# Half of an output projection moved into the delta rule's prologue, with partial sums kept in DRAM

## The chip, the core and the metric

The kernel runs on one core of a Trainium2 chip. The metric is the device time of one execution in microseconds (us). Engines: PE is TensorE (PEld its weight loads), DVE VectorE, ACT ScalarE, POOL GpSimd, and SP SyncE, which here only issues transfers; each of them takes its instructions in the order in which the program has them.

## What is computed

Block one mixes a sequence of 512 latent positions (and 256 context positions) with a state space part (SSD) and a gated delta rule (GDN), and ends with an output projection, a norm and a gated residual. Block two starts from that. Cut to what matters here:

```
def merge(ssd_y, gdn_o, z, dtype):
    y = jnp.concatenate([ssd_out_norm(ssd_y, z[..., :SSD_WIDTH], ssd_norm_w),
                         gdn_out_norm(gdn_o, z[..., SSD_WIDTH:], gdn_norm_w)], axis=-1)
    return rms_norm(y.astype(dtype) @ w_out, post_w)
h_lat = h_lat + gate_l[:, None] * merge(ssd_l, gdn_l, z_l, h_lat.dtype)
...
hn = rmsnorm(h, e_norm[j])
u = hn @ e_w_in[j]
```

D is 2048. The first 1024 rows of `w_out` meet the SSD half of y, the last 1024 rows the GDN half. SSD is finished before GDN begins.

## The kernel before

**Stages.** The program is a row of stages with a barrier of all engines between them: `ssd_stage`, then `gdn_stage` (from 1076.7 us of the span), then `even_stage` (from 1459.2 us), whose first part is block one's output projection. Tiles are [128 partitions, ...]; y lies in DRAM as 16 blocks of 128 channels x 512 positions, 256 KB each (`y1[0:8]` from SSD, `y1[8:16]` from GDN).

**The projection.** `Projection` computes jobs: a job is 128 output columns, a sum over KD = 16 steps of 128 rows. Operands are split into a high and a low part, so that a step is three matmuls of 128x512: hi*hi, hi*lo, lo*hi. Weights come in chunks of four steps (128x512, 256 KB), through a ring of buffers: SP loads chunk m into `w`, ACT writes the high part `w_hi` (`split_high`, which waits for the load and for PE to be done with the chunk one ring before), DVE subtracts to get `w_lo` (`split_low`), PE multiplies and counts `chunk_done`. Two PSUM accumulators alternate, so job n can start only when job n-2 was evacuated.

**even_stage** has 16 such jobs called "mix" (`MixedInput` holds what surrounds them), with a ring of 8. SP's order is in `MixedInput.load`: chunks and the 16 y blocks, alternating, through a ring of four y buffers, then `h` (4 MB), two tables, then the further chunks. ACT and DVE split each y block (`x_hi`, `x_lo`), and PE waits for block k in job 0. For each job ACT first runs `split_high` 8 chunks ahead of the job's last chunk, then squares the accumulator and copies it times a gain into `mixed[n]`; DVE sums the squares in `total`. A matmul with ones turns it into the norm (`pe_mixed`), and then DVE goes over the 16 blocks: mixed*inv, h+mixed, and the low part of u, block by block, with block two's first three jobs behind it on PE.

**gdn_stage** handles eight heads in four pairs. Its prologue prepares the first two heads (`norms`, `turn_v`, `turn_k`, `products` on PE, `squares`, `norms`, `decay`, `copy`, `queries` on ACT, `norms`, `decayed` on DVE), squares and norms of heads 2 and 3, and a triangular inverse of 96 blocks of 32x32: SP gathers them through DRAM (`gather`, `blocks_load`), DVE runs 31 dependent steps (`triangle`), ACT transposes (`turn_tri`), SP writes them out and spreads them (`scatter`, 4 and 16 transfers). PE's first matmul of the main loop (`level5_t`, L361) waits for the spread. From there the four pairs run; they are not touched by the change.

How far the three engines run ahead of PE is in `sp_upto`, `act_upto` and `dve_upto`: at step s SP loads chunks up to s's chunk + 2*ring and stores every job that is done, ACT splits up to s's chunk + ring and then evacuates the jobs that are done, DVE subtracts up to s's chunk + ring. Since a split of chunk m waits for PE to be done with chunk m-ring, an engine that is asked for `chunk(s) + ring` stands still until PE has come to step s.

## Time and profile before

| | us |
|---|---|
| runs (3) | 4012.24, 4014.65, 4020.4; median 4014.65 |
| profiled execution, span from first to last instruction | 4017.9 |
| PE busy in it | 3635.5 (90%) |
| DVE busy | 1998.8 (50%) |
| ACT busy | 1513.7 (38%) |
| prologue of gdn_stage, first instruction to first L361 | 1076.7 to 1163.6 |
| mix part of even_stage, first matmul to last | 1464.2 to 1658.3 |

The profiled execution is listed with its span only; a time of its own beside it is not given, and the span lies within the three runs. Busy PE means that some matmul is in the array or its end is modelled there; what a matmul costs in a dense row is read from their count over a stretch, not from the duration of one. Times on the trace are from the start of the span.

### The profile page before, as it was taken

How to read it: one execution, taken by the hardware profiler on the slowest of the kernel's cores; microseconds unless marked ns; L12 is line 12 of the kernel's file. 1: busy time of each engine (PE TensorE's matmuls, PEld its weight loads, DVE VectorE, ACT ScalarE, POOL GpSimd, SP SyncE). 2: the span in 40 equal slices, each digit the busy share in tenths (PEclk: the TensorE clock that was granted, in tenths of full speed). 3: DMA queues.
4: the chain of work that ended last, by engine and by line, in shares of the span. 5: the costliest groups of instructions: out<-in, count | busy, mean ns of one | idle time of the engine just before them, and what ended most of it. 6: DMA issues, size and time to landing. Idle time of an engine off the chain costs nothing. (4 is left out here: it accounts for less than half of the span.)

```text
span 4017.9 us, 50439 instructions
## 1 busy us (share of the span) xinstructions
PE 3635.5 (90%) x20182; PEld 2995.2 (75%) x20182; DVE 1998.8 (50%) x3101; ACT 1513.7 (38%) x2512; POOL 430.6 (11%) x334
## 2 busy tenths in 40 slices
PE   6699999899647679999999879999999899989998
PEld 2288888787546558778888768787899788867786
DVE  6554555464567533555555553445533344444454
ACT  1322222244545343455655642323222344432332
POOL 1000000042221000011101140020000000013011
PEclk8899999899878889999999989999999999999999
DMA  9344343223232253233322253335755667633332
GB/s 353 123 159 130 103 134 108 87 54 104 97 100 83 64 160 102 89 111 90 94 84 82 61 160 97 92 97 90 121 118 116 103 107 105 108 87 115 92 91 88
DMA packets 585417, 437.91 MB, mean 109 GB/s; under 512 B 63734, under 2 KB 519874, under 8 KB 583904
## 3 DMA queue, kind: packets, MB, share of 16 engines
q1 hardware_dynamic: 578272, 414.88, 39.4%
q10 hardware_dynamic: 6048, 19.14, 1.2%
q8 instruction: 159, 2.61, 0.3%
q0 software_dynamic: 864, 0.67, 0.1%
q14 instruction: 74, 0.61, 0.0%
HBM read 381.31 MB, written 53.26 MB: 108 GB/s over the span
## 5 line engine op out<-in xcount | busy, mean ns | idle before, releaser
L1913 DVE TENSOR_TENSOR w_lo<-w,w_hi 128x512 fp32r<-128x512 f32 x446 | 303.7, 697 | 598.3 <-ACT w_hi L1906 598.3
L1906 ACT ACTIVATE w_hi<-w 128x512 fp32r<-128x512 f32 x446 | 272.8, 626 | 586.0 <-PE od_acc L1892 177.5
L3670 PE MATMUL ta_acc<-ta_x_hi,w_hi 128*128 128x512 f32 x1024 | 404.5, 395 | 13.6 <-DVE ta_x_lo L3810 8.2
L3780 DVE TENSOR_TENSOR w_lo<-w,w_hi 128x512 fp32r<-128x512 f32 x260 | 207.4, 800 | 407.2 <-ACT w_hi L3698 405.5
L3671 PE MATMUL ta_acc<-ta_x_lo,w_hi 128*128 128x512 f32 x1024 | 401.8, 392 | 0.0
L3672 PE MATMUL ta_acc<-ta_x_hi,w_lo 128*128 128x512 f32 x1024 | 401.4, 392 | 0.0
L3698 ACT ACTIVATE w_hi<-w 128x512 fp32r<-128x512 f32 x260 | 164.1, 631 | 507.0 <-PE ta_acc L3672 474.9
L1890 PE MATMUL od_acc<-od_u_hi,w_hi 128*128 128x512 f32 x768 | 306.1, 399 | 11.3 <-DVE w_lo L1913 10.5
L1890 PE MATMUL ev_acc<-ev_u_hi,w_hi 128*128 128x512 f32 x680 | 282.6, 416 | 31.2 <-DVE ev_u_lo L2637 19.7
L1892 PE MATMUL od_acc<-od_u_hi,w_lo 128*128 128x512 f32 x768 | 300.4, 391 | 0.0
L1891 PE MATMUL od_acc<-od_u_lo,w_hi 128*128 128x512 f32 x768 | 300.3, 391 | 0.0
L1891 PE MATMUL ev_acc<-ev_u_lo,w_hi 128*128 128x512 f32 x680 | 269.6, 396 | 0.0
L1892 PE MATMUL ev_acc<-ev_u_hi,w_lo 128*128 128x512 f32 x680 | 268.9, 396 | 0.0
L3670 PEld LDWEIGHTS ta_acc<-ta_x_hi,w_hi 128*128 128x128 f32 x1024 | 194.2, 190 | 55.5 <-issue 12.0
L1377 PE MATMUL p_acc<-u_hi,p_w_hi 128*128 128x512 f32 x576 | 228.4, 396 | 7.5 <-DVE p_w_lo L1489 7.5
L1384 PE MATMUL p_acc<-u_hi,p_w_lo 128*128 128x512 f32 x576 | 228.6, 397 | 0.0
L1378 PE MATMUL p_acc<-u_lo,p_w_hi 128*128 128x512 f32 x576 | 225.0, 391 | 0.0
L3672 PEld LDWEIGHTS ta_acc<-ta_x_hi,w_lo 128*128 128x128 f32 x1024 | 194.3, 190 | 41.1
L3671 PEld LDWEIGHTS ta_acc<-ta_x_lo,w_hi 128*128 128x128 f32 x1024 | 194.3, 190 | 40.5 <-issue 0.5
L1534 DVE TENSOR_TENSOR p_w_lo<-p_w,p_w_hi 128x1024 fp32r<-128x1024 f32 x68 | 83.0, 1223 | 242.6 <-ACT p_w_hi L1432 242.6
L1890 PEld LDWEIGHTS ev_acc<-ev_u_hi,w_hi 128*128 128x128 f32 x680 | 130.3, 192 | 72.5 <-DVE w_lo L1913 14.6
L1890 PEld LDWEIGHTS od_acc<-od_u_hi,w_hi 128*128 128x128 f32 x768 | 145.2, 189 | 44.5 <-DVE w_lo L1913 11.3
(640 smaller groups left out, 8081.8 us busy)
## 6 DMA issues: line engine op xcount, KB each, us to landing
w<-in_o_w_in_dram SPq DMA_DIRECT2D x260, 256.0 KB, 8.1
p_w<-in_w_in_dram SPq DMA_DIRECT2D x72, 512.0 KB, 4.9
w<-in_e_w_in_dram SPq DMA_DIRECT2D x144, 256.0 KB, 2.9
mod_w<-in_w_ada_dram SPq DMA_DIRECT2D x8, 4096.0 KB, 23.9
w<-in_ple_gate_w_dram SPq DMA_DIRECT2D x128, 256.0 KB, 2.8
gate_w<-in_w_ada_dram SPq DMA_DIRECT2D x16, 1024.0 KB, 6.0
z_w<-in_w_in_dram SPq DMA_DIRECT2D x64, 256.0 KB, 2.9
w<-in_e_w_out_dram SPq DMA_DIRECT2D x64, 256.0 KB, 2.8
```

What stands on the lines that cost most here:

```text
L1377: pe.matmul(lat, wh, x_hi[:, k, :], start=first, stop=False)
L1378: pe.matmul(lat, wh, x_lo[:, k, :], start=False, stop=False)
L1384: last = pe.matmul(lat, wl, x_hi[:, k, :], start=False, stop=end)
L1890: pe.matmul(out, hi, self.x_hi[:, k, :], start=first, stop=False)
L1891: pe.matmul(out, hi, self.x_lo[:, k, :], start=False, stop=False)
L1892: last = pe.matmul(out, lo, self.x_hi[:, k, :], start=False, stop=end)
L1906: act.activation(self.w_hi[m % self.ring][:], self.w[m % self.ring][:], ACT.Copy).then_inc(self.hi_set, 1)
L1913: eng.tensor_tensor(self.w_lo[m % self.ring][:], self.w[m % self.ring][:], self.w_hi[m % self.ring][:].bitcast(F32), ALU.subtract).then_in ...
L3670: pe.matmul(bank, hi, hi_x[:, k, :], start=(k == 0), stop=False)
L3671: pe.matmul(bank, hi, lo_x[:, k, :], start=False, stop=False)
L3672: last = pe.matmul(bank, lo, hi_x[:, k, :], start=False, stop=(k == job.kd - 1))
L3780: dve.tensor_tensor(w_lo[m % RING][:], w[m % RING][:], w_hi[m % RING][:].bitcast(F32), ALU.subtract).then_inc(lo_set, 1)
```

## The change

Eight of the 16 steps of every mix job, those for the SSD half of y, leave even_stage and go into gdn_stage's prologue, as 16 jobs of 8 steps called `mix` (a second `Projection`, with a ring of 4 and the banks 0 and 1). PE does them in portions between the prologue's parts (`MIX_AT` gives the step up to which it goes at each place). ACT evacuates each of these jobs into `mx_out`, SP stores it to a DRAM tensor `mix_part` (16 x 256 KB). In even_stage the 16 blocks of `mix_part` are loaded into `mixed[n]`, DVE adds the accumulator of the other 8 steps to them, ACT squares the sum, and the gain moves into the later multiplication on DVE. The y tiles, weight buffers and outputs of the new jobs lie where `y_m1`, `qdec2`, `qdec3`, `z_in` and others lie later, so these loads and a memset now stand behind the last store. The prologue's operations themselves are the same.

```diff
+MIX = KD // 2
+MIX_AT = (8, 16, 24, 32, 40, 48, 56, 72, MIX * KD)
...
+        with ExitStack() as early:
+            def split(part):
+                return early.enter_context(nc.sbuf_tensor(f"mx_y_{part}", [P, MIX, LAT], F32R))
+
+            y_hi, y_lo = split("hi"), split("lo")
+            y_in = [early.enter_context(nc.sbuf_tensor(f"mx_y_in{i}", [P, LAT], F32)) for i in range(2)]
+            mix = Projection(nc, early, "mx", (y_hi, y_lo),
+                             [Job("plain", w_mix, P * n, mix_part[n], stores=True, kd=MIX) for n in range(KD)],
+                             4, None, acc=[[bank[0]], [bank[1]]], ahead=4)
+            mix.buffers(nc, early, "mx")
...
+        def by_job(upto, eng, step):
+
+            while eng_at[upto.__name__] < step:
+                eng_at[upto.__name__] = min(step, (eng_at[upto.__name__] // MIX + 1) * MIX)
+                upto(eng, eng_at[upto.__name__])
+
+        eng_at = {"sp_upto": 0, "act_upto": 0}
+        mix_at = dict(zip(("norms", "v0", "k0", "kq0", "v1", "k1", "kq1", "sums", "rest"), MIX_AT))
...
+            def load_y(k):
+                if k >= 2:
+                    sp.wait_ge(mix.x_set, k - 1)
+                sp.dma_start(y_in[k % 2][:], y_ready[k]).then_inc(y_loaded[k % 2], 16)
+
             for hd in range(2):
                 load_kq(hd)
+            mix.load_weights(sp, 1)
...
+            for k in range(2):
+                load_y(k)
+            mix.load_weights(sp, 4)
             for hd in range(2):
                 load_qdec(hd)
             for hd in range(2, 4):
...
-            load_z(0)
+            for k in range(2, MIX):
+                load_y(k)
+            by_job(mix.sp_upto, sp, mix_at["kq0"])
             gather(0)
             load_kq(2)
             load_v(2)
+            by_job(mix.sp_upto, sp, mix_at["kq1"])
             gather(1)
             blocks_load(0)
             load_kq(3)
             load_v(3)
+            by_job(mix.sp_upto, sp, mix_at["rest"])
+            mix.wait_stored(sp)
+            load_z(0)
             for hd in range(2, 4):
                 load_qdec(hd)
...
             norms(0)
+            mix.pe_upto(pe, mix_at["norms"])
             for hd in range(2):
                 turn_v(hd)
+                mix.pe_upto(pe, mix_at[f"v{hd}"])
                 turn_k(hd)
+                mix.pe_upto(pe, mix_at[f"k{hd}"])
                 products(hd)
-            norms(1)
+                mix.pe_upto(pe, mix_at[f"kq{hd}"])
+            norms(1, lambda: mix.pe_upto(pe, mix_at["sums"]))
+            mix.pe_upto(pe, mix_at["rest"])
...
+            def split_y(ks):
+                for k in ks:
+                    act.wait_ge(y_loaded[k % 2], 16 * (k // 2 + 1))
+                    act.activation(y_hi[:, k, :], y_in[k % 2][:], ACT.Copy).then_inc(y_hi_set, 1)
+
             squares(0)
             squares(1)
+            mix.split_high(act, 1)
+            split_y(range(2))
             norms(0)
+            mix.split_high(act, 2)
+            split_y(range(2, MIX))
+            mix.act_upto(act, 0)
             decay(0)
             copy(0, v_tok[0], v_turned, v_copied)
+            by_job(mix.act_upto, act, mix_at["v0"])
             copy(0, k_tok[0], k_turned, k_copied)
-            decay(1)
-            copy(1, v_tok[1], v_turned, v_copied)
-            copy(1, k_tok[1], k_turned, k_copied)
+            by_job(mix.act_upto, act, mix_at["k0"])
             queries(0)
             queries(1)
+            decay(1)
+            by_job(mix.act_upto, act, mix_at["kq0"])
+            copy(1, v_tok[1], v_turned, v_copied)
+            by_job(mix.act_upto, act, mix_at["v1"])
+            copy(1, k_tok[1], k_turned, k_copied)
+            by_job(mix.act_upto, act, mix_at["k1"])
+            by_job(mix.act_upto, act, mix_at["kq1"])
             squares(2)
             squares(3)
+            by_job(mix.act_upto, act, mix_at["sums"])
             norms(1)
-            decay(2)
-            decay(3)
+            for hd in (2, 3):
+                for half in range(2):
+                    decay(hd, range(3 * half, 3 * half + 3))
+                    by_job(mix.act_upto, act, mix_at["sums"] + 12 * (2 * (hd - 2) + half + 1))
+            by_job(mix.act_upto, act, mix_at["rest"])
+            mix.wait_stored(act)
             turn_tri(0)
...
+            mix.split_low(dve, 1)
+            split_y(range(2))
             norms(0)
+            mix.split_low(dve, 2)
+            split_y(range(2, 4))
             norms(1)
+            split_y(range(4, MIX))
+            mix.dve_upto(dve, mix_at["v0"])
+            mix.dve_upto(dve, mix_at["kq0"])
             decayed(0)
+            mix.dve_upto(dve, mix_at["k1"])
             decayed(1)
+            mix.dve_upto(dve, mix_at["sums"])
             for n in range(TRI_STEPS):
                 triangle(0, n)
+                mix.dve_upto(dve, mix_at["sums"] + (n + 1) * (mix.total - mix_at["sums"]) // TRI_STEPS)
             norms(2)
             norms(3)
+            mix.dve_upto(dve, mix.total)
+            dve.wait_ge(mix.chunk_done, len(mix.chunks))
+            mix.wait_stored(dve)
+            dve.memset(y_m[1][:], 0.0).then_inc(cleared, 1)
...
-        self.load_weights(sp, self.chunks_at(step) + 2 * self.ring)
+        self.load_weights(sp, self.chunks_at(step) + self.ahead)
...
+        for k in range(MIX):
+            proj.load_weights(sp, min(proj.ring, k + 1))
             if k >= 4:
                 sp.wait_ge(self.y_set, k - 3)
             sp.dma_start(self.y_ring[k % 4], self.y_dram[k]).then_inc(self.y_in[k % 4], 16)
         proj.load_weights(sp, proj.ring)
+        for n in range(self.lead):
+            sp.dma_start(self.mixed[n], self.mix_part[n]).then_inc(self.part_in[n // 4], 16)
         sp.dma_start(self.h[:], self.h_dram.rearrange("b p t -> p b t")).then_inc(self.h_in, 16)
...
-            bank = proj.accumulator(n)[0]
-            act.wait_ge(proj.chunk_done, proj.chunk_end[n])
+            act.wait_ge(proj.evacuated, n + 1)
             if n >= 3:
                 act.wait_ge(self.mix_added, n - 2)
-            act.activation(self.total if n == 0 else self.sq[n % 2], bank[:, :], ACT.Square).then_inc(self.mix_sq, 1)
-            act.activation(self.mixed[n], bank[:, :], ACT.Copy, scale=self.post_gain[:, n:n + 1]).then_inc(proj.evacuated, 1)
+            act.activation(self.total if n == 0 else self.sq[n % 2], self.mixed[n], ACT.Square).then_inc(self.mix_sq, 1)
...
+        def squared(n):
             if n > 0:
                 dve.wait_ge(self.mix_sq, n + 1)
                 if n > 1:
                     dve.wait_ge(self.mix_added, n - 1)
                 dve.tensor_tensor(self.total, self.total, self.sq[n % 2], ALU.add).then_inc(self.mix_added, 1)
+
+        for n in range(self.lead):
+            proj.split_low(dve, proj.chunk_end[n] + proj.ring)
+            dve.wait_ge(self.part_in[n // 4], 64)
+            dve.wait_ge(proj.chunk_done, proj.chunk_end[n])
+            dve.tensor_tensor(self.mixed[n], self.mixed[n], proj.accumulator(n)[0][:, :], ALU.add).then_inc(proj.evacuated, 1)
+            if n > 0:
+                squared(n - 1)
+        squared(self.lead - 1)
...
-            dve.tensor_tensor(self.mixed[k], self.mixed[k], self.inv[:], ALU.mult).then_inc(self.mix_normed, 1)
+            dve.scalar_tensor_tensor(self.mixed[k], self.mixed[k], self.post_gain[:, k:k + 1], self.inv[:], ALU.mult, ALU.mult
+                                     ).then_inc(self.mix_normed, 1)
...
-                jobs.append(Job("mix", w_mix, P * n))
+                jobs.append(Job("mix", w_mix, P * n, k_first=MIX, kd=MIX))
```

`by_job` walks to a step in pieces of one job, so that on SP loads for two chunks alternate with one store. The other hunks give `Job` a first row and a number of steps, and replace `KD * n` by `plan.start(n)`.

**SP in the prologue.** Names: `gdn_qdec`, `gdn_a_t` and `gdn_z_in` are loads of gdn_stage, `s_blocks_in` the gather, `s_blocks_out` the write that follows the triangle. Before:

```order
L200 DMA gdn_qdec<-s_cum_rows 128x1024 x2
L194 DMA gdn_a_t<-s_cum_rows 128x1536 x2
L204 DMA gdn_z_in<-s_z 128x2x512
L214 DMA s_blocks_in<-gdn_a_t 32x6x32 x4
L214 DMA s_blocks_in<-gdn_a_turned 32x6x32 x4
...
L200 DMA gdn_qdec<-s_cum_rows 128x1024 x2
L229 DMA s_blocks_out<-gdn_tri 48x1024
```

and with the change, from the weights `mx_w` and y blocks `mx_y_in` on (`s_mix_part` is the store of a job):

```order
L221 DMA gdn_a_t<-s_cum_rows 128x1536 x2
L274 DMA mx_y_in<-s_y 128x512 x6
L1925 DMA mx_w<-in_w_out_dram 128x4x128 x2
...
L241 DMA s_blocks_in<-gdn_a_t 32x6x32 x4
L241 DMA s_blocks_in<-gdn_a_turned 32x6x32 x4
...
L1925 DMA mx_w<-in_w_out_dram 128x4x128 x2
L1939 DMA s_mix_part<-mx_out 128x512
...
L1939 DMA s_mix_part<-mx_out 128x512 x3
L231 DMA gdn_z_in<-s_z 128x2x512
L227 DMA gdn_qdec<-s_cum_rows 128x1024 x2
L256 DMA s_blocks_out<-gdn_tri 48x1024
```

Four stores and eight chunk loads stand ahead of the first gather, three more pairs ahead of the second, and z and two qdec loads, issued early before, stand behind the last store and ahead of `s_blocks_out`.

**ACT in the prologue**, from the last norm exponential of heads 0 and 1 on. Before:

```order
L523 ACTIVATE gdn_sq_q<-gdn_sq_q,gdn_ln_scale 128x512
L534 ACTIVATE gdn_a_t<-gdn_a_t,gdn_ncum 128x128 x12
L527 ACTIVATE gdn_v_tok<-gdn_bank 128x512
L528 ACTIVATE gdn_v_tok<-gdn_bank 128x256
L527 ACTIVATE gdn_k_tok<-gdn_bank 128x512
L528 ACTIVATE gdn_k_tok<-gdn_bank 128x256
L534 ACTIVATE gdn_a_t<-gdn_a_t,gdn_ncum 128x128 x12
```

and with the change (`mx_w_hi` is split_high, `mx_y_hi` the high part of a y block, `mx_out` the evacuation of a job):

```order
L572 ACTIVATE gdn_sq_q<-gdn_sq_q,gdn_ln_scale 128x512
L1999 ACTIVATE mx_w_hi<-mx_w 128x512
L662 ACTIVATE mx_y_hi<-mx_y_in 128x512 x6
L1999 ACTIVATE mx_w_hi<-mx_w 128x512 x2
L583 ACTIVATE gdn_a_t<-gdn_a_t,gdn_ncum 128x128 x12
L576 ACTIVATE gdn_v_tok<-gdn_bank 128x512
L577 ACTIVATE gdn_v_tok<-gdn_bank 128x256
L1999 ACTIVATE mx_w_hi<-mx_w 128x512 x2
L2015 ACTIVATE mx_out<-gdn_bank 128x512
L1999 ACTIVATE mx_w_hi<-mx_w 128x512 x2
L2015 ACTIVATE mx_out<-gdn_bank 128x512
L576 ACTIVATE gdn_k_tok<-gdn_bank 128x512
```

Six y blocks stand ahead of the first decay row, and two jobs' splits and evacuations ahead of the copy of k.

**SP at the start of even_stage.** `ev_raw` and `ev_mixed` are the y ring. Before:

```order
L1832 DMA ev_w<-in_w_out_dram 128x4x128
L2585 DMA ev_mixed<-s_y 128x512 x2
L2587 DMA h<-s_h 128x16x512
L2838 DMA k_scan<-in_c_scan_dram 128x768
L2838 DMA k_start<-in_c_start_dram 128x512
L1832 DMA w<-in_w_out_dram 128x4x128 x6
```

and with the change, where the rows on `s_mix_part` fill the `mixed` tiles:

```order
L1925 DMA ev_w<-in_w_out_dram 128x4x128
L2679 DMA ev_mixed<-s_y 128x512
L2682 DMA ev_sn<-s_mix_part 128x512 x4
L2682 DMA ev_v_tok<-s_mix_part 128x512 x4
...
L2682 DMA p_tok<-s_mix_part 128x512
L2683 DMA h<-s_h 128x16x512
L2945 DMA k_scan<-in_c_scan_dram 128x768
L2945 DMA k_start<-in_c_start_dram 128x512
L1925 DMA w<-in_w_out_dram 128x4x128 x6
```

The 16 loads of partial sums stand between the last y block and h, and chunk 8 stands behind both.

## Rows read from the trace of the kernel before

**Rows 1.** Windows: length, busy us (count) of PE, PEld, DVE, ACT, POOL, PEclk, DMA share, GB/s.

```profile
1076.00:1164.00 88.00, 30.09 (x120) 19.25 (x124) 50.39 (x106) 40.12 (x88) 20.41 (x10) 0.62 0.45 141
...
1082.00:1097.00 15.00, 8.13 (x20) 3.96 (x20) 8.06 (x5) 11.72 (x27) 7.87 (x4) 0.73 0.98 377
...
1520.00:1560.00 40.00, 40.00 (x176) 32.89 (x176) 11.49 (x17) 12.42 (x21) 0.00 (x0) 1.00 0.33 95
```

**Rows 2.** Timeline of PE in gdn_stage: start, us, instruction, wait before.

```profile
1163.55 1.51 PE L361 MATMUL gdn_bank<-gdn_x_m,gdn_a_t 32*32 32x32 f32 x96 [31.69 <-DMA gdn_y_m<-s_blocks_out]
...
1172.30 1.16 PE L337 MATMUL gdn_bank<-gdn_q_n,gdn_k_n 128*128 128x128 f32 x8
1173.29 1.50 PE L344 MATMUL gdn_bank<-gdn_k_n 128*128 128x128 f32 x12
...
1176.27 0.87 PE L315 MATMUL gdn_bank<-k_ident,gdn_raw_v 128*128 128x128 f32 x6
```

**Rows 3.** Part 6 and part 5 of the page: median us to landing; busy, mean ns.

```profile
w<-in_w_out_dram SPq DMA_DIRECT2D x48, 256.0 KB, 2.9
...
h<-s_h SPq DMA_DIRECT2D x2, 4096.0 KB, 16.4
...
s_y<-gdn_o SPq DMA_DIRECT2D x8, 256.0 KB, 3.0
...
L1913 DVE TENSOR_TENSOR w_lo<-w,w_hi 128x512 fp32r<-128x512 f32 x446 | 303.7, 697 | 598.3 <-ACT w_hi L1906 598.3
L1906 ACT ACTIVATE w_hi<-w 128x512 fp32r<-128x512 f32 x446 | 272.8, 626 | 586.0 <-PE od_acc L1892 177.5
```

**Rows 4.** Timeline of SP (issues) in gdn_stage's prologue.

```profile
1107.45 1.79 SPq L214 DMA_DIRECT2D s_blocks_in<-gdn_a_t  x4
1109.28 2.16 SPq L214 DMA_DIRECT2D s_blocks_in<-gdn_a_turned  x4
...
1120.49 0.32 SPq L220 DMA_DIRECT2D gdn_blk<-s_blocks_in  x1
...
1121.32 0.43 SPq L184 DMA_DIRECT2D gdn_k_n<-s_qkv  x1
...
1149.34 0.33 SPq L229 DMA_DIRECT2D s_blocks_out<-gdn_tri  x1
```

**Rows 5.** Timeline of ACT in the same prologue.

```profile
1099.03 3.60 ACT L534 ACTIVATE gdn_a_t<-gdn_a_t,gdn_ncum 128x128 f32<-128x128 f32 x12
...
1126.37 0.84 ACT L509 ACTIVATE gdn_sq_k<-gdn_k_n 128x768 f32<-128x768 f32 x1 [9.65 <-DMA gdn_k_n<-s_qkv]
...
1147.24 2.02 ACT L544 ACTIVATE gdn_blk<-gdn_tri 96x1024 f32<-96x1024 f32 x1 [4.96 <-DVE gdn_tri L746]
```

**Rows 6.** Timelines of DVE and POOL in the same prologue.

```profile
1090.47 3.37 DVE L702 TENSOR_TENSOR gdn_k_n<-gdn_k_n,gdn_sq_k 128x768 f32<-128x768 f32 x1 [5.45 <-ACT gdn_sq_k L521]
...
1094.37 0.94 DVE L702 TENSOR_TENSOR gdn_k_n<-gdn_k_n,gdn_sq_k 128x768 f32<-128x768 f32 x1
...
1101.38 1.22 DVE L710 TENSOR_TENSOR gdn_attn<-gdn_bank,gdn_a_t 128x1024 f32<-128x1024 f32 x1 [5.47 <-PE gdn_bank L337]
...
1106.44 0.98 DVE L724 STREAM_TRANSPOSE gdn_a_turned<-gdn_a_t 128x768 f32<-128x768 f32 x1
...
1108.66 4.67 POOL L663 TENSOR_TENSOR gdn_qdec<-gdn_qdec,gdn_q_n 128x1024 f32<-128x1024 f32 x2 [14.53 <-ACT gdn_qdec L540]
1113.29 6.81 POOL L658 TENSOR_TENSOR gdn_a_t<-gdn_a_t,k_neg 128x1536 f32<-128x1536 f32 x2
```

**Rows 7.** Timelines of SP, PE and DVE in even_stage's mix part and behind it.

```profile
1478.77 0.44 SPq L2587 DMA_DIRECT2D h<-s_h  x1
...
1502.18 0.79 PE L1890 MATMUL ev_acc<-ev_u_hi,w_hi 128*128 128x512 f32 x1 [4.45 <-ACT ev_sn L2608]
...
1660.37 1.73 PE L2676 MATMUL ev_misc_bank<-p_tok,k_ones 128*128 128x512 f32 x2 [2.11 <-DVE p_tok L2644]
...
1666.34 0.74 DVE L2652 SCALAR_TENSOR_TENSOR ev_u_lo<-h,cols,ev_u_hi 128x512 fp32r<-128x512 f32 x1
```

More of the change, by code:

```diff
@@ L290, in _, with norms @@
         def _(pe):
[L291 removed]
+            def norms(p, between=None):
                 first, second = 2 * p, 2 * p + 1
@@ L1879, in pe_steps @@
             hi, lo = self.w_hi[m % self.ring][:, here], self.w_lo[m % self.ring][:, here]
-            first, end = k == 0, k == KD - 1
+            first, end = k == 0, k == job.kd - 1
             if job.kind == "tok":
@@ L2595, in act @@
         act.preload_act_table_set(EXP_LN)
-        for k in range(KD):
+        for k in range(MIX):
             if k % 4 == 0:
```

92 lines of the change are left out of this document (53 added, 39 removed).

## The prediction

> **What bounds the kernel now.** I read the windows by stage first, then the timelines of each engine in the two stretches that the change touches. PE is busy for 90% of the span, but not evenly. In the mix part of even_stage it is dense: 176 matmuls in 40 us at full granted clock [rows 1], 0.227 us each, 0.684 us for a step of three. So eight steps less in a job are worth what they take there. In gdn_stage's prologue PE is busy for 30 us of 88 [rows 1], and its first matmul of the main loop waits 31.7 us for the spread of the triangle's blocks [rows 2]. The chain there runs over SP, DVE and DMA: gather, 31 triangle steps, transpose, write, spread. The change puts 128 steps, 128 x 0.684 = 87.6 us of PE, into a stretch that has 58 us of idle PE, 16 of which (the write and spread) lie behind all of it. The question is how much longer the prologue gets.
>
> **even_stage.** Before, PE gets through jobs 0 and 1 (32 steps), then stands until 1502.2, because job 2 needs job 0 evacuated, and ACT evacuates only after it has split chunks that stand behind h in SP's queue [rows 7]. From 1502.2 it does 224 steps. After, jobs 0 and 1 are 16 steps, the same wait stands behind them, and 112 steps are left:
> - 112 steps x 0.684 = 76.6 us removed.
> - The restart moves. The y phase is 8 blocks shorter: h was issued at 1478.8 [rows 7], and the partial sums can be issued from about 1471 (half the y blocks, the same eight chunks). Their 4.2 MB take between 11.1 us (377 GB/s, the densest stretch [rows 1]) and 16.4 (the 4 MB load of h [rows 3]). So h goes 3.3 to 8.6 us later than before, and so does the restart. I take 4, near the rate, because these rows follow each other in one queue.
> - Behind the last matmul DVE's addition stands ahead of the square: 0.7 us (a 128x512 operation is 0.70 [rows 3]). It was 2.1 us from last matmul to the sum [rows 7].
> - The gain in the multiplication turns 16 tensor operations of 0.70 into scalar_tensor_tensor ones of 0.74 [rows 3, 7], on DVE, which paces that stretch: 0.7, with rounding 1.
>
> In a job of 5.5 us DVE has two splits, two additions (2.8 us) and ACT two splits and a square (1.9): both fit. Sum: -76.6 + 4 + 0.7 + 1 = **-70.9**, with -74 and -66 as bounds.
>
> **The prologue: PE's ledger.** I follow PE from its first job.
> - Job 0 needs all eight y blocks. Ahead of y2 SP has put 7.8 MB; at 377 GB/s [rows 1] from about 1079 they are in at 1100. The ring of two then turns three more times: issue to landing 2.9, split 0.63, subtraction 0.70 [rows 3], some 4.4 us a pair. The last part is there at 1111.4, job 0 ends at **1112.1**.
> - The other 15 jobs: 15 x 8 x 0.684 = **82.1** us, if PE stays at full clock.
> - The prologue's own work behind job 0: four turns at 0.9 and two products at 2.5 [rows 2], the norm sums of heads 2 and 3, some 4.5 by the same pace: **13.1**.
> - Waits that the order makes, **16.1** in all:
>  (a) 4.7 before the second turn of v. DVE is asked for chunk 11 before `decayed(0)`, so it starts that only after job 3 has ended (1132.9) and ACT and DVE have split; it starts at 1136.2, and v's turn waits for its first operation, 1.2 us [rows 6].
>  (b) 2.8 before the second products. The gather waits for all of `decayed(0)` (6.0 us from 1101.4 to 1107.4 [rows 6]), issues for 4.0 [rows 4], then three loads; only then chunk 12 is issued (1147.8), 2.9 to land, two splits, an evacuation, and the copy of k, which stands behind them on ACT. Jobs 4 and 5 and two turns cover 12.8 of this.
>  (c) 2.2 before the norm sums: `squares(2)` stands behind the evacuation of job 6.
>  (d) 6.4 in the middle of the norms: `squares(3)` needs k of head 3, which SP issues behind the second gather and `blocks_load` (it landed 5.0 us after its issue [rows 4, 5]); chunks 18 to 21 are behind it, and the norm logarithms behind job 8's evacuation. Jobs 7 and 8 cover 10.9.
> - PE ends the last job at 1112.1 + 82.1 + 13.1 + 16.1 = **1223.4**. In that dense end ACT (two splits, an evacuation, 1.8 us of decay [rows 5] and a turn of SP of 0.45 + 0.9 + 2.9) just keeps the pace of 5.5 us a job, and the triangle is spread over it.
> - Behind it, serial: evacuation 0.7, store 3.0 [rows 3], transpose 2.0 [rows 5], and what lay between the first write of blocks and L361, 1163.6 - 1149.3 = 14.2 [rows 2, 4]; z and two qdec loads, 1.6 MB, now stand ahead of the write, of which some 0.7 show behind the transpose. **20.6**.
>
> So L361 comes at 1244.0 where it came at 1163.6: +80.4. I add 1.6 for two things. After a wait of 4 to 6 us the granted clock is low for the next matmuls: before its mix part resumes, 4.5 us of waiting end in a first matmul of 0.79 us [rows 7]; (a) and (d) are such waits, up to 2.5 us each, and the waits behind hide some. And DVE can stand behind POOL: `k_n` took 3.37 us while POOL worked and 0.94 us without [rows 6], 2.4 late. POOL's two queries and two arguments (11.5 us in a row [rows 6]) fall on DVE's splits of chunks 10 and 11, which (a) hangs on. Bounds 0 to 9. **Prologue +82**, bounds 76 to 92.
>
> The Trainium skill ("SBUF — State Buffer", section "SBUF: two separate sides") says that DVE with two SBUF inputs and POOL exclude each other for a whole instruction. The trace agrees for `k_n` [rows 6]. By that rule both splits could be held for a full argument of 3.4 us each, +6.8 in place of the 1.6; the sum would be +16 in place of +11.
>
> **Sum.** 82 - 70.9 = **+11 us**. From the median of the three runs, 4014.65: **4026**; the profiled span, 4017.9, would become 4029. What a measurement of this kernel can tell from no change is about 0.2%, 8 us.
>
> **Rivals.**
> 1. *PE packs the prologue* (other side). If ACT, DVE and SP are never late for PE, waits (a) to (d) and the 1.6 go: 11 - 16.1 - 1.6 = -7, and if y2 doesn't stand behind 3.4 MB of loads (it lands as the chunks of [rows 3] do) another 5 fall away: -12, 4003. It decides when less than 5 us of the waits and extras are left over. For it: (b) and (c) are differences of long sums, and ACT is busy for only 40 of 88 us before [rows 1]. Against: (a) and (d) are waits of an in-order engine behind named instructions, not for want of time. Chance 0.17.
> 2. *About even.* The waits come out at half, or the partial sums load inside the time that the y blocks free: +11 - 8 = +3, 4018, between 4007 and 4022.7. For it: one term of 8 us out of six is enough. Chance 0.31.
> 3. *SP's turn sets the pace.* A store, two loads and their landing make 0.45 + 0.9 + 2.9, with splits and evacuation 5.3 us a job, against 5.5 for PE. If transfers land after 4 us instead of 2.9, as the longer ones do [rows 4, 5], the turn is 6.4 and each of the nine last jobs costs 0.9 more: +8 on top, 4034, and with the shared port of DVE and POOL 4039. Chance 0.16, inside "slower".
> 4. *It doesn't shorten even_stage as said.* If the 16 loads take h's 16.4 us, the restart is 8.6 late and the stage gains 66: +16, 4031. Chance 0.1, inside "slower".
>
> **How the numbers follow.** Slower by over 0.2% (my forecast with 0.26, rivals 3 and 4): 0.52. Within 0.2%: 0.31. Faster: 0.17. The forecast is the likeliest single case, 4026, with its own range of 4018 to 4036. The range that leaves out 2 in 10 goes from 4004 (most of rival 1 lies above) to 4038 (rival 3 without the port).
>
> **What the profile after would show.** First L361 at 1244 to 1246 (rival 1: some 1223, rival 3: 1254). Job 0's last matmul at 1112. PE waits named by DVE `gdn_attn` (a), ACT `gdn_k_tok` (b), ACT `gdn_sq_k` (c, d). From the last mix matmul to L361 some 20 us of idle PE. In even_stage, measured from its first instruction, PE's restart at +48 us in place of +43, the last mix matmul at +126 in place of +199. The main loop of gdn_stage and all behind the mix part are as long as before. The prediction is wrong if the order's waits are covered (1), if landing takes longer in the prologue (3), or if the granted clock stays low there: at half the clock over the first four jobs PE would lose 20 us more.

## The result, and the profile after

| | before | changed |
|---|---|---|
| median of the runs on one chip | 4017.53 us (4 runs, 4012.24 to 4023.57) | 4047.91 us (4 runs, 4047.54 to 4051.15) |
| profiled span, granted clock | 4017.9 us, 0.950 | 4045.9 us, 0.948 |

The ratio is 1.0074, 95% interval 1.0061 to 1.0088: the changed kernel is slower by 30 us. The forecast was 4026, within 4004 to 4038. One more execution of the changed kernel, on another chip, took 4043.12 us, 23 us above that chip's 4020.05 (median of 21 runs of before). So the difference is known to some 23 to 30 us.

I cut both spans at the same instructions of PE: the prologue from the first norm sums to the first matmul of level 5 (`level5_t`), the main loop from there to even_stage's first matmul, and even_stage's mix part from there to the sum behind the mix (L2676 before, L2779 after). Each stretch is a difference of two start times in PE's timeline. The last two columns are the repeats of both kernels, made for the experiments below.

| us | before | changed | difference | before again | changed again |
|---|---|---|---|---|---|
| prologue | 81.96 | 178.41 | +96.5 | 81.86 | 177.07 |
| main loop | 300.65 | 307.40 | +6.8 | 304.18 | 304.86 |
| even_stage's mix part | 196.17 | 120.35 | -75.8 | 196.11 | 121.06 |

So even_stage gave back a little more than forecast (70.9), the prologue grew by 14 more than forecast (82), and the main loop, which was to stay, came out 7 longer in this pair of executions.

PE's timeline of the changed kernel; columns are start, duration, instruction, and in brackets the idle time before it and what ended it:

```profile
1146.04 1.51 PE L359 MATMUL gdn_bank<-k_ident,gdn_raw_v 128*128 128x128 f32 x6 [10.76 <-DVE gdn_attn L779]
...
1162.79 1.78 PE L381 MATMUL gdn_bank<-gdn_q_n,gdn_k_n 128*128 128x128 f32 x8 [2.66 <-ACT gdn_k_tok L577]
...
1174.41 1.12 PE L340 MATMUL gdn_bank<-gdn_sq_k,k_ones 128*128 128x512 f32 x2 [2.00 <-ACT gdn_sq_k L558]
...
1196.56 1.22 PE L353 MATMUL gdn_bank<-gdn_sq_k,k_ones 128*128 128x256 f32 x2 [7.93 <-ACT gdn_sq_k L566]
...
1260.57 1.50 PE L405 MATMUL gdn_bank<-gdn_x_m,gdn_a_t 32*32 32x32 f32 x96 [21.97 <-DMA gdn_y_m<-s_blocks_out]
...
1605.47 0.79 PE L1983 MATMUL ev_acc<-ev_u_hi,w_hi 128*128 128x512 f32 x1 [19.40 <-DVE ev_sn L2743]
...
1688.32 1.64 PE L2779 MATMUL ev_misc_bank<-p_tok,k_ones 128*128 128x512 f32 x2 [3.50 <-DVE p_tok L2737]
```

The first four are waits (a), (b), (c) and (d) of the forecast, at the instructions it named. (b) and (c) have the forecast size (2.7 and 2.0 for 2.8 and 2.2), (d) is 7.9 for 6.4, and (a) is 10.8 instead of 4.7. The fifth answers to the 31.7 us of [rows 2]: 22.0 for the forecast 20.6. What stands behind (a) shows on DVE and POOL:

```profile
1132.17 4.73 POOL L733 TENSOR_TENSOR gdn_qdec<-gdn_qdec,gdn_q_n 128x1024 f32<-128x1024 f32 x2 [37.10 <-ACT gdn_qdec L589]
1136.85 7.25 POOL L728 TENSOR_TENSOR gdn_a_t<-gdn_a_t,k_neg 128x1536 f32<-128x1536 f32 x2
...
1137.03 7.62 DVE L2006 TENSOR_TENSOR mx_w_lo<-mx_w,mx_w_hi 128x512 fp32r<-128x512 f32 x2 [5.71 <-ACT mx_w_hi L1999]
1144.57 1.21 DVE L779 TENSOR_TENSOR gdn_attn<-gdn_bank,gdn_a_t 128x1024 f32<-128x1024 f32 x1
```

DVE's two splits of chunks 10 and 11, 0.7 us each elsewhere, take 7.6 together and end just after POOL's two arguments do (1144.1). In the two other executions of this prologue (changed again, prologue alone) they took 7.67 and 7.64 us, and wait (a) was 8.5 and 9.6 us, shorter because PE reached it later. PE's clock behind the waits is in the windows (the columns behind the colon are length, busy time by engine with count, granted clock, DMA share, GB/s):

```profile
1146.04:1153.86 7.82, 7.82 (x31) 6.50 (x31) 3.95 (x13) 0.87 (x2) 0.00 (x0) 0.78 0.13 21
1162.79:1172.41 9.62, 9.62 (x44) 8.29 (x44) 5.92 (x16) 2.38 (x4) 0.00 (x0) 0.82 0.53 164
```

The first holds the turn of v and job 4, the second the products and job 6, both without a gap and at a mean granted clock of 0.78 and 0.82, so partly at the lower level of 1.2 GHz. How much that costs, kernel 9 below shows, in which the same work stands behind no wait.

### The profile page after: what moved, and what is told of

Its sections match the earlier page's. It is cut to its first block and busy times, and to the rows that moved or that the text cites. A ratio compares the mean times of both kernels' runs of the same rounds, so it can differ in the third digit from the quotient of the medians.

```text
span 4045.9 us, 50530 instructions
## 1 busy us (share of the span) xinstructions
PE 3637.0 (90%) x20182; PEld 2997.1 (74%) x20182; DVE 2012.4 (50%) x3117; ACT 1513.1 (37%) x2512; POOL 431.4 (11%) x334
## 5 line engine op out<-in xcount | busy, mean ns | idle before, releaser
L2006 DVE TENSOR_TENSOR w_lo<-w,w_hi 128x512 fp32r<-128x512 f32 x422 | 287.1, 698 | 559.7 <-ACT w_hi L1999 559.4
L1999 ACT ACTIVATE w_hi<-w 128x512 fp32r<-128x512 f32 x422 | 257.4, 626 | 544.2 <-PE od_acc L1985 164.7
L3887 DVE TENSOR_TENSOR w_lo<-w,w_hi 128x512 fp32r<-128x512 f32 x260 | 206.4, 796 | 408.3 <-ACT w_hi L3805 406.7
L3805 ACT ACTIVATE w_hi<-w 128x512 fp32r<-128x512 f32 x260 | 164.1, 631 | 507.0 <-PE ta_acc L3779 474.9
L1983 PE MATMUL od_acc<-od_u_hi,w_hi 128*128 128x512 f32 x768 | 306.1, 399 | 11.2 <-DVE w_lo L2006 10.0
L1983 PE MATMUL ev_acc<-ev_u_hi,w_hi 128*128 128x512 f32 x584 | 245.2, 420 | 42.8 <-DVE ev_sn L2743 19.4
L1984 PE MATMUL ev_acc<-ev_u_lo,w_hi 128*128 128x512 f32 x584 | 232.3, 398 | 0.0
L1985 PE MATMUL ev_acc<-ev_u_hi,w_lo 128*128 128x512 f32 x584 | 231.6, 397 | 0.0
L1983 PEld LDWEIGHTS od_acc<-od_u_hi,w_hi 128*128 128x128 f32 x768 | 145.1, 189 | 44.2 <-DVE w_lo L2006 10.8
L1520 ACT ACTIVATE p_w_hi<-p_w 128x1024 fp32r<-128x1024 f32 x68 | 71.9, 1061 | 264.8 <-PE p_acc L1472 198.2
```

Source lines behind the costliest of these rows:

```text
L1983: pe.matmul(out, hi, self.x_hi[:, k, :], start=first, stop=False)
L1984: pe.matmul(out, hi, self.x_lo[:, k, :], start=False, stop=False)
L1985: last = pe.matmul(out, lo, self.x_hi[:, k, :], start=False, stop=end)
L1999: act.activation(self.w_hi[m % self.ring][:], self.w[m % self.ring][:], ACT.Copy).then_inc(self.hi_set, 1)
L2006: eng.tensor_tensor(self.w_lo[m % self.ring][:], self.w[m % self.ring][:], self.w_hi[m % self.ring][:].bitcast(F32), ALU.subtract).then_in ...
L3887: dve.tensor_tensor(w_lo[m % RING][:], w[m % RING][:], w_hi[m % RING][:].bitcast(F32), ALU.subtract).then_inc(lo_set, 1)
```

## Experiments

The three stretches of a row are from one profiled execution, cut as above; the median is that of the kernel's 4 to 11 runs, and the ratio is to the kernel before, run on the same chip. The rows were made on three chips (1 to 4; 5 to 7; 8 to 10), and apart from its repeat the changed kernel was not run on them, so medians are compared across these groups, and with its 4047.91, only roughly. Two profiled executions are the slowest of their kernel's 11 runs: "both repairs" took 4031.10 us in it (median 4020.48, the next slowest 4024.49), "before, loads held" 4019.15 (median 4012.47).

| kernel | prologue | main loop | mix part | median us | ratio (95%) |
|---|---|---|---|---|---|
| GpSimd later | 172.87 | 303.30 | 120.74 | 4036.74 | 1.0048 (1.0033 to 1.0063) |
| decayed(0) first | 163.71 | 306.34 | 119.35 | 4028.98 | 1.0026 (1.0014 to 1.0039) |
| prologue alone | 177.49 | 308.10 | 195.71 | 4122.46 | 1.0259 (1.0243 to 1.0274) |
| even stage alone | 81.99 | 304.24 | 120.75 | 3934.99 | 0.9791 (0.9777 to 0.9806) |
| waits | 161.21 | 303.82 | 120.58 | 4026.24 | 1.0019 (1.0011 to 1.0028) |
| scatter early | 156.38 | 311.59 | 119.96 | 4027.96 | 1.0013 (1.0003 to 1.0022) |
| both repairs | 153.26 | 314.83 | 121.17 | 4020.48 | 1.0001 (0.9993 to 1.0010) |
| loads held | 149.84 | 304.41 | 120.99 | 4016.48 | 0.9993 (0.9983 to 1.0002) |
| all repairs | 144.28 | 299.99 | 120.50 | 4001.88 | 0.9950 (0.9936 to 0.9963) |
| before, loads held | 81.79 | 301.05 | 196.09 | 4012.47 | 0.9980 (0.9971 to 0.9989) |

**1. GpSimd later: is it the port?**

```diff
             identity(0)
+            pool.wait_ge(attn_set, 1)
             queries(0)
```

> GpSimd waits for the first attn_set before its two queries and the arguments of heads 2 and 3, so none of it stands beside VectorE's splits of chunks 10 and 11; the rest is the changed kernel. Shared port of VectorE and GpSimd (my theory for 6 of the 10.8 us of wait (a)): the two splits take 0.7 us each in place of 7.6, wait (a) falls to about 4.7 us, and the whole comes out 6 us shorter, 4042. Rival, the splits are late for ScalarE's high parts or the slow clock: wait (a) stays at 10 us and the time within 2 us of 4048.

The prologue is 5.5 us shorter, and the median is 4036.74 us where 4042 was expected (the main loop came out 4.1 shorter in this execution too). DVE and POOL of this kernel:

```profile
1134.01 0.69 DVE L2007 TENSOR_TENSOR mx_w_lo<-mx_w,mx_w_hi 128x512 fp32r<-128x512 f32 x1 [5.72 <-ACT mx_w_hi L2000]
1135.23 0.69 DVE L2007 TENSOR_TENSOR mx_w_lo<-mx_w,mx_w_hi 128x512 fp32r<-128x512 f32 x1 [0.52 <-ACT mx_w_hi L2000]
...
1137.09 3.19 DVE L787 SCALAR_TENSOR_TENSOR gdn_a_t<-gdn_bank,gdn_tabs,gdn_a_t 128x128 f32<-128x128 f32 x12
...
1137.13 4.72 POOL L733 TENSOR_TENSOR gdn_qdec<-gdn_qdec,gdn_q_n 128x1024 f32<-128x1024 f32 x2 [45.94 <-DVE gdn_attn L780]
```

Both splits are back at 0.69 us: they took 6.2 us longer beside POOL. Wait (a) is 2.84 us instead of 10.76. Of these 7.9 us, 6.2 are the splits; the rest is that PE came later to the wait itself (its job 3 ended 55.9 us behind the first norm sums, 53.1 in the changed kernel; the granted clock was 0.50 from 1101.0 to 1112.7). The cause of the splits' delay is shown: POOL stood in DVE's way. The clock's part stayed: behind a wait of 2.84 us the turn of v and job 4 still took 7.5 us at 0.81, and the products and job 6 took 9.4 at 0.84.

The third row is a finer reading. POOL works beside the twelve operations of `decayed`, which take one operand from PSUM, and they need 3.19 us as they do without it. Here that is POOL's multiplication of queries; in before it was the argument as well, the instruction that held the splits:

```profile
1111.38 3.19 DVE L717 SCALAR_TENSOR_TENSOR gdn_a_t<-gdn_bank,gdn_tabs,gdn_a_t 128x128 f32<-128x128 f32 x12 [0.48 <-PE gdn_bank L344]
...
1113.29 6.81 POOL L658 TENSOR_TENSOR gdn_a_t<-gdn_a_t,k_neg 128x1536 f32<-128x1536 f32 x2
```

So it is DVE's operations with both tensor operands in SBUF that are held. By the rule of the Trainium skill ("SBUF — State Buffer", section "SBUF: two separate sides") that the prediction weighed, that is what should happen; the trace agrees in both directions.

**2. decayed(0) first: is (a) the order's doing?**

```diff
-            mix.dve_upto(dve, mix_at["kq0"])
+            mix.dve_upto(dve, mix_at["k0"])
             decayed(0)
```

> VectorE is asked for the chunks only up to 9 before it starts decayed(0), and splits chunks 10 and 11 behind it; the rest is the changed kernel. If wait (a) is the order's doing: it disappears (under 1 us), the first gather starts some 8 us earlier, and TensorE's last job of the mix ends 10.8 us earlier: 4037. Rival, SP's turn or ScalarE takes the place (waits (b) and (d) grow by what (a) loses): 4044 to 4048.

Wait (a) is gone and the prologue is 14.7 us shorter, 4 more than the wait itself. The two splits are as slow as before (7.82 us, POOL's arguments beside them), but now nothing waits for them: PE works on jobs 4 and 5 from chunks already split. The 4 us more are mostly the clock: from PE's turn of v to its turn of k, with job 4 between, it is 6.1 us here (1133.84 to 1139.95) and 7.8 in the changed kernel; the products and job 6 take 8.0 and 9.6. (b) and (d) keep their sizes (3.1 and 7.7), so the rival, that they grow by what (a) loses, falls. The median, 4028.98, is 8 us below the 4037 expected, more than these 4 us explain.

Only the first 1.7 of these us belong to wait (a), though. The window of the products and job 6 stands behind wait (b), 3.06 us here, and its granted clock is 1.00:

```profile
1149.28:1157.25 7.97, 7.97 (x44) 6.66 (x44) 4.62 (x12) 1.88 (x4) 0.00 (x0) 1.00 0.64 196
```

In the changed kernel, its repeat, kernel 1 and the prologue alone the same work behind a (b) of 2.3 to 3.1 us had 0.82 to 0.84 and took 9.4 to 9.6 us, and so it had in kernel 6, which has no wait (a) either (a (b) of 4.05 us, 0.82, 9.6 us). So behind (b) five of six executions show the lower level in part, and kernel 2's is the exception, by which its profile looks 1.6 us better than the repair made it.

**3 and 4. Each half alone: do the parts add up?** The first kernel has the changed prologue and before's even_stage; the second has no job in the prologue and the halved even_stage.

> The prologue of the changed kernel (all 16 jobs, their stores, its SBUF layout) with the even stage of before: the whole output projection is done there again, and the partial sums are written and not read. Additive theory: prologue +96.3 and main loop +6.7 as in the changed kernel, so 103 us above before, 4121. If the 6.7 us of the main loop is chance of one execution: 4114. Rival, the stages share something (clock, DMA): over 4 us away from both.

> The halved even stage alone: gdn_stage has the changed kernel's SBUF layout and order but no job of the mix; the even stage loads a block of h in place of each partial sum, so the output lacks the first half of the projection. Theory: 75.6 us below before plus at most 1, so 3942, prologue as before within 2 us. The main loop of gdn_stage tells the 6.7 us apart: 302 us if the SBUF layout makes it, 295.6 if the work ahead of it (clock or placement of its instructions) does.

The prologue alone costs 103 us (4122.46 - 4019.41), as expected to a microsecond. The even stage alone gives 75.4 us in its own stretch, but the whole is 84 lower: 9 more than the theory has, and the parts don't add up to the changed kernel (103 - 84 is 19, not 30). Most of the 9 us lie far behind the change, in the odd stage, where PE has 10 us of idle time in the 100 us from 1400 to 1500 behind the mix's last sum in before and in the changed kernel, and 3 here. The data are other ones there, since this kernel's output lacks half a projection, and I did not follow it up; the price of the even stage is read from its own stretch. For the main loop this kernel was to show 302 or 295.6 us and showed neither: with the new layout and without jobs it took 304.2, as before's own repeat did, so no length can be put down to the layout.

**5. Waits (b), (c), (d).** On top of kernel 2:

```diff
             by_job(mix.sp_upto, sp, mix_at["kq0"])
+            mix.load_weights(sp, 14)
             gather(0)
...
+            load_kq(3)
+            load_v(3)
             gather(1)
             blocks_load(0)
-            load_kq(3)
-            load_v(3)
...
-            by_job(mix.act_upto, act, mix_at["kq1"])
             squares(2)
+            by_job(mix.act_upto, act, mix_at["kq1"])
             squares(3)
```

> On top of the kernel with decayed(0) first: SyncE issues chunks 12 and 13 before the first gather and the loads of head 3 before the second gather, and ScalarE takes squares(2) ahead of the splits and the evacuation behind it. In that kernel TensorE's waits were (b) 3.1, (c) 2.6 and (d) 7.7 us. If each is the order's doing: all three fall under 1 us, the last job of the mix ends 12 us earlier, and the time is 4016 (ratio 1.000 to before). Rival, the triangle or SyncE's turn then sets the end: the gap from the last matmul of the mix to the main loop grows by what they save, and 4022 to 4028 comes out.

The time is 4026.24 where 4016 was expected. That is the rival's number, but not by its mechanism: the gap from the last job to the main loop stayed at 21.7 us. (b) and (c) are gone as foreseen, but (d) grew from 7.7 to 9.8, and the prologue is only 2.5 shorter. The forecast had put (d) down to `squares(3)` first. That is now done at 1162.1, and PE still waits until 1177.9. ScalarE's timeline shows for what:

```profile
1169.52 1.38 ACT L2000 ACTIVATE mx_w_hi<-mx_w 128x512 fp32r<-128x512 f32 x2 [7.38 <-DMA mx_w<-in_w_out_dram]
1170.81 0.58 ACT L2016 ACTIVATE mx_out<-gdn_bank 128x512 f32<-128x512 f32 x1
1174.95 0.63 ACT L2000 ACTIVATE mx_w_hi<-mx_w 128x512 fp32r<-128x512 f32 x1 [3.55 <-DMA mx_w<-in_w_out_dram]
1175.74 0.63 ACT L2000 ACTIVATE mx_w_hi<-mx_w 128x512 fp32r<-128x512 f32 x1 [0.16 <-DMA mx_w<-in_w_out_dram]
1176.27 0.58 ACT L2016 ACTIVATE mx_out<-gdn_bank 128x512 f32<-128x512 f32 x1
1176.75 1.04 ACT L567 ACTIVATE gdn_sq_k<-gdn_bank,gdn_eps 128x512 f32<-128x512 f32 x2
```

The logarithms (L567) that PE needs stand behind two evacuations and four splits, and the splits wait for chunks 18 to 21, which SP issues behind the second gather. What was forecast as the second cause of (d) is the one that ends last.

**6 and 7. The serial tail.** The triangle is spread over jobs 9 to 13 (8 to 13 in kernel 7), its transposition, write and spread stand behind job 13, z and the queries' decays behind them, and VectorE does the first pair's `level5_x` ahead of the keys. Kernel 6 has this on top of kernel 2, kernel 7 on top of kernel 5, with GpSimd's arguments behind the split of chunk 11 as well.

```diff
-            by_job(mix.sp_upto, sp, mix_at["rest"])
-            mix.wait_stored(sp)
-            load_z(0)
-            for hd in range(2, 4):
-                load_qdec(hd)
-            scatter(0)
+            by_job(mix.sp_upto, sp, mix_at["rest"] - 2 * MIX)
+            scatter_out(0)
+            scatter_in(0)
+            by_job(mix.sp_upto, sp, mix_at["rest"])
+            mix.wait_stored(sp)
+            load_z(0)
+            for hd in range(2, 4):
+                load_qdec(hd)
```

> On top of the kernel with decayed(0) first: the triangle is done by job 13, the transposition and the whole write and spread stand behind job 13 instead of behind job 15 and its store, z and the queries' decays load behind them; VectorE does level5_x of the first pair ahead of the keys. If the 21.6 us behind the last matmul are only a serial tail: the gap from the last matmul of the mix to the first instruction of the main loop falls to 4 to 8 us, and the time is 15 us lower, 4014. Rival, the triangle can't be had earlier or SyncE's 16 spread issues hold the last chunks: the last job of the mix ends later by what the tail saves, 4025 or more.

> Both of the above, and GpSimd's arguments of heads 2 and 3 wait until the split of chunk 11 is done. If the ledger of waits holds, 12 and 15 us add up: 4002, ratio 0.996 to before, main loop starting 50 to 56 us later than in before. Rival, VectorE can't have the triangle's 21 us and the splits done when job 13 ends: the tail is 12 us and 4010 comes out.

Neither kernel comes down to its forecast (4014 and 4002, measured 4027.96 and 4020.48). The gap between PE's last mix matmul and the main loop falls from 22 to 11.2 and 11.9 us, less than expected, since in kernel 7 it is still 17.6 us from job 13's store (1218.1) to the main loop (1235.7), with PE's last two jobs beside only the first 6. And in the profiled executions the main loop got longer by much of what the prologue saved: 312 and 315 us. The excess is in the first pair (84.3 and 87.9 us from `level5_t` to `level5_t`, 79 to 81 in all kernels without this edit), at one wait, which no instruction ends. First kernel 6, then kernel 7:

```profile
1248.14 2.83 PE L442 MATMUL gdn_bank<-gdn_x_m,gdn_a_t 64*64 64x64 f32 x48 [4.22 <-issue]
...
1246.79 2.82 PE L443 MATMUL gdn_bank<-gdn_x_m,gdn_a_t 64*64 64x64 f32 x48 [4.31 <-issue]
...
1240.31 2.31 DVE L833 TENSOR_SCALAR gdn_x_m<-gdn_bank 32x384 f32<-32x384 f32 x4 [19.07 <-PE gdn_bank L424]
...
1237.12 0.37 SPq L231 DMA_DIRECT2D gdn_z_in<-s_z  x1
1237.54 1.58 SPq L227 DMA_DIRECT2D gdn_qdec<-s_cum_rows  x2
```

In kernel 7 DVE's block was ready at 1242.6, and PE started 4.2 us later. The 1.5 MB of z and decays, loads that stood ahead of the main loop in the kernels above, kept the DMA engines busy to 0.92 in the 2.5 us before this wait and to 0.80 in its first 1.5 us, but to 0.05 in its last 2.8. So PE stood on after most of the transfers were over. In both kernels it started some 9.5 us after SP had issued z. The wait costs more than its length: behind it the granted clock was 0.50, and the 48 matmuls took 2.8 us where they take 1.6 in the other kernels.

**8. Loads held.** Kernel 7, with z and the decays behind level 6 of the first pair:

```diff
             mix.wait_stored(sp)
+            sp.wait_ge(y6_ready, 2)
             load_z(0)
```

> The kernel with both repairs, in which the main loop's first pair took 87.9 us in place of 79 to 81: TensorE stands 4.3 us at the first matmul of level 6, 4.1 us after VectorE's block was ready, while z and two loads of the queries' decays (1.5 MB) are in the DMA engines. Here SyncE holds these three loads until level 6 of the first pair is issued. Theory, TensorE's own instructions are fetched behind these loads: that wait falls under 1 us, the pair takes 81 to 84 us and the time is 4 to 6 us lower, 4015. Rival, the wait is of another kind (a block of VectorE, the clock): it stays, 4020.

```profile
1239.44 1.61 PE L444 MATMUL gdn_bank<-gdn_x_m,gdn_a_t 64*64 64x64 f32 x48 [1.23 <-DVE gdn_x_m L834]
```

The wait without a releaser is gone, the same matmuls take 1.61 instead of 2.82 us, and the pair takes 79.95 us. Two kernels with the loads in this place have the wait (4.2 and 4.3 us), and the two in which they are held, this one and the next, don't have it. So the wait hangs on these loads. That PE's own instructions are fetched behind them is a reading that would fit (the profile calls the wait "issue", and nothing else in the chain was late); no row shows the fetch, and another cause isn't ruled out. What it is worth in time isn't shown: the medians of kernels 7 and 8 differ by 4 us and their intervals overlap, and the 18 us between their profiled executions are those between kernel 7's slowest run and the second fastest of kernel 8; 3.4 us of them lie in the prologue, ahead of the edit.

**9. All repairs.**

```diff
+            norms(1, (0,))
             squares(3)
             by_job(mix.act_upto, act, mix_at["sums"])
-            norms(1)
+            norms(1, (1, 2))
...
             load_v(3)
+            mix.load_weights(sp, 20)
             gather(1)
...
+            by_job(mix.sp_upto, sp, mix_at["rest"] - 3 * MIX)
+            mix.load_weights(sp, 32)
             scatter_out(0)
+            by_job(mix.sp_upto, sp, mix_at["rest"] - 2 * MIX)
             scatter_in(0)
```

> All repairs: ScalarE takes the first head's three logarithms ahead of the evacuations (wait (d)), chunks 18 and 19 are issued before the second gather, the triangle is spread over jobs 8 to 12, its transposition and write stand behind job 12 and the spread behind job 13, and the bulk loads of z and of the queries' decays wait for level 6 in every pair. If waits and serial tail are what made the prologue long: the main loop starts 60 us later than in before instead of 96, it takes 300 us, and the time is 3998, ratio 0.995. Rival, TensorE's 88 us of matmuls can't be fed in this stretch (a turn of SyncE, VectorE's triangle): main loop 70 us later and 4010.

4001.88 us, ratio 0.995: faster than both kernels. No wait of over 1.3 us is left on PE between job 0 and the last job. The main loop starts 62 us later than in before (60 expected). The rival was partly right too: SP gets to write the triangle only at 1212.3, for which it had been given job 12's end, and PE stands 11 us behind its last mix matmul. The two windows that answer to those of the changed kernel (the same instructions, same counts but for a record or two):

```profile
1135.21:1141.32 6.11, 6.11 (x31) 5.11 (x30) 2.74 (x5) 3.57 (x11) 4.64 (x2) 1.00 0.40 122
1147.43:1155.14 7.71, 7.71 (x45) 6.74 (x44) 3.36 (x7) 3.00 (x5) 0.00 (x0) 1.00 0.57 186
```

At full granted clock they take 6.1 and 7.7 us; behind the waits they took 7.8 and 9.6. So the lower clock behind waits (a) and (b) cost another 3.6 us; with a wait (a) of only 2.8 us (experiment 1) 3.1 of them are still lost. Behind (d) the changed kernel's granted clock was 0.50 as well, for 4.0 us of dense work:

```profile
1196.56:1200.60 4.04, 4.04 (x8) 2.54 (x9) 0.58 (x3) 2.65 (x5) 0.00 (x0) 0.50 0.62 186
```

That is up to 2.0 us more (half of it, an estimate; no run has this work at full clock).

**10. Before, with the loads held.** Is this gain the mix's at all? The kernel before, where only SP's loads of decays and z in the main loop are moved behind level 6 of the next pair:

```diff
-                if ahead:
-                    load_qdec(2 * j + 4)
-                    load_qdec(2 * j + 5)
                 sp.wait_ge(y_set, 2 * (j + 1))
...
+                if more:
+                    sp.wait_ge(y6_ready, 2 * (j + 2))
+                if ahead:
+                    load_qdec(2 * j + 4)
+                    load_qdec(2 * j + 5)
                 if more:
                     load_z(j + 1)
```

> The kernel before with only this edit: in the main loop SyncE issues the loads of the queries' decays and of z behind level 6 of the next pair instead of ahead of it. Theory, TensorE's stalls without a releaser (2.1, 2.0 and 1.8 us, in levels 5 of pairs 1 and 2) are instruction fetches behind these loads: they go, the main loop takes 294 to 297 us in place of 300.7 to 304.2, and the time is 4 to 6 us lower than before, ratio 0.9985. Rival, they are of another kind: ratio 1.000.

The time is 7.6 us lower, ratio 0.998, so the rival (1.000) falls. But the profiled main loop is 301.05 us where 294 to 297 was expected. PE's stalls in before:

```profile
1249.44 0.71 PE L385 MATMUL gdn_bank<-gdn_y_m,gdn_t 32*32 32x32 f32 x59 [2.08 <-issue]
...
1329.51 0.60 PE L374 MATMUL gdn_bank<-gdn_t,gdn_y_m 32*32 32x32 f32 x28 [1.98 <-issue]
...
1333.24 0.32 PE L385 MATMUL gdn_bank<-gdn_y_m,gdn_t 32*32 32x32 f32 x4 [1.84 <-issue]
```

and in this kernel:

```profile
1248.94 0.71 PE L387 MATMUL gdn_bank<-gdn_y_m,gdn_t 32*32 32x32 f32 x59 [1.19 <-issue]
...
1329.79 0.32 PE L387 MATMUL gdn_bank<-gdn_y_m,gdn_t 32*32 32x32 f32 x4 [1.66 <-issue]
```

Two got shorter and one went: 3 of 5.9 us, and 1.2 and 1.7 us remain with the DMA engines idle beside them (share 0.00), so bulk loads are not their only cause. The main loop took 300.65 and 304.18 us in before's two profiles. The effect is in the measured times, but this execution, the slowest of 11, shows only the 3 us of it. Since the kernel with all repairs holds these loads too, the moved mix with its repairs is worth 18.2 - 7.6 = 11 us, 0.3%, on the same chip. Its reordered first pair (`level5_x` ahead of the keys) wasn't tried alone in before.

**Two repeats.**

> The kernel before, once more, for how far one profiled execution differs from another. gdn_stage's main loop took 300.7 us from its first matmul to that of the next stage in before, 307.4 in the changed kernel, 303 to 308 in its variants. If one execution's chance makes this: 300 to 308 here. If it belongs to the kernel: 300.7 within 1 us.

> The changed kernel once more, for how far one execution differs from another. The main loop took 307.4 us in the first profile; before took 300.7 and 304.2 in two. Chance: 303 to 308 here. If the change itself makes the loop longer: 306.5 or more.

Before's loop took 304.18, the changed kernel's 304.86, beside 300.65 and 307.40 the first time. One and the same kernel thus differs by 3.5 and 2.5 us, and 0.7 us is what separates the second two. The six executions that have jobs in the prologue and SP's old order behind it took 303.3 to 308.1 us, 305.6 in the mean. Part of this is in the same three stalls without a releaser: 5.9 and 6.0 us in before's two profiles, 8.0 and 7.2 in the changed kernel's. Why they are longer there no run shows; whether the change adds one or a few microseconds stays open.

## Why the prediction was wrong

The direction was right, the size was not (11 forecast, 30 measured). By its own steps:

- **even_stage, -70.9**: measured -75.8 up to the sum behind the mix (-75.1 in the two repeats). The 112 steps held. The restart of PE was to come 4 us later (+48) and came at 42.6 behind the stage's first instruction, where before had 43.0. SP issued the first partial sum 10.9 us into the stage (forecast 12) and h at 18.5 (19.6 before): the eight y blocks that fell away made room for all 16 partial sums, whose issue took 7.6 us, and their 4.2 MB did not show behind it. The term should have been 0. The step from the last matmul to the sum was +1.4 (forecast +0.7), and the scalar_tensor_tensor forms, which lie behind this cut, cost 0.2 us (from the sum to the first matmul on `ev_scores` of the attention 78.2 us before, 78.4 after) for a forecast of 1.
- **Job 0 at 1112.1**: 1115.1, of which 0.8 is the stage's later start in this execution. 2 us missed.
- **Waits (b), (c), (d), 11.4 us**: 12.6. (b) and (c) were right in place and size. (d) was nearly right in size; of the two causes given, the logarithms behind job 8's evacuation ended last (experiment 5), not `squares(3)`.
- **Wait (a), 4.7 us, and the 1.6 us for clock and port**: this is the step that failed. The mechanisms were right, the term was far too small. The prediction had seen both mechanisms and named their place: POOL's 11.5 us on DVE's splits of chunks 10 and 11, and the clock behind (a) and (d). It gave both together 1.6. The wait came out 6.1 us longer, with the two splits 6.2 us longer beside POOL (experiment 1), and the clock took 3.6 behind (a) and (b) (experiment 9): 9.7 us in place of 1.6, beyond even the bound of 9, and up to 2.0 more behind (d). In the repeat, in which (a) was 8.5 us, it is 3.8 and 3.8, 7.6 together, and what came behind (d). The rule of the Trainium skill ("SBUF — State Buffer", section "SBUF: two separate sides") gave +6.8 for the port, and the splits lost 6.2. It was set aside as if the overlap in time were a matter of luck, though it follows from the order: POOL's queries wait for ScalarE's exponentials, and the arguments follow at once, for 12 us in all, and (a) is PE's only wait for DVE between job 0 and the last job. The clock was looked for behind (a) and (d), with up to 2.5 us each, about what it cost there (1.7 and up to 2.0); behind (b), where nothing was expected, it cost 1.9.
- **Tail, 20.6 us**: 22.0. SP could issue the spread only at 1251.0, 5.4 us after the last write of blocks (2.6 in before, 2.8 in kernels 6 and 7, in which z and the decays come behind), since z and the decays were ahead of these writes.
- **Main loop, 0**: +6.8 in the first pair of profiles, +0.7 in the second. The range of 4004 to 4038 was built from the terms alone and had no room for it. That alone doesn't explain the miss: without the 6.8 us the kernel would have been at 4041, still outside the range.

Sum in its own terms: 82 + 14.5 in the prologue, -70.9 - 4.9 in even_stage, +6.8 in the loop, +0.6 ahead of the first norm sums, gives +28.1 (the spans differ by 28.0). The 14.5 and the 0.6 are, by the terms above, 3.0 for job 0, 8.1 for port and clock up to (b), up to 2.0 for the clock behind (d), 1.2 for (b) to (d) themselves and 1.4 for the tail, up to 15.7 together. That the miss isn't larger is luck: even_stage was off by 4.9 us the other way.

Of the rivals, "PE packs the prologue" described what all repairs together made of it, not this kernel. "SP's turn sets the pace" didn't come: jobs 9 to 15 took 40.1 us for a forecast of 38.3. "It doesn't shorten even_stage as said" is refuted.

## What to carry to other kernels

Work put into an idle stretch doesn't cost what its matmuls cost, but what the in-order engines around it make of it: here 88 us of PE cost 96, although the stretch had 58 us of idle time, and with the same work in another order 62. Before such a move, list for each engine what stands ahead of the instruction that the busiest engine waits for, and ask where the serial tail at the end of the stretch could start earlier: together this was worth 34 us of prologue, three times what the move in the end gave. When two mechanisms are seen to fall on the one wait that matters, price them in full.
